# A decode-and-prompt hybrid layer: sample queries computed as rows, a third key place from the start, scores half a sample further ahead, gate sigmoids after the sample loop

## What is computed

```python
h = rms_norm(x, g_norm1) * (1.0 + sc1) + sh1
proj = h @ w_in        # q|k|v (8 heads x 64), glu_a|glu_b (512 each), gate_a|gate_c (1024 each)
q = rms_norm(q.reshape(B, S, 8, 64), g_q)      # k likewise with g_k
attn = moba_attention(q, k_all, v_all, pos0, alibi_slopes()) @ w_attn_proj   # top-3 past blocks of 256 keys, plus the own block
u = glu_a * sigmoid(glu_b)
cv = silu(layer_norm(depthwise_conv31(u))) @ w_conv_proj
mix = (sigmoid(gate_a) * attn + sigmoid(gate_c) * cv) @ w_out
x = x + gt1 * mix
# then: second norm, SwiGLU with 2816 hidden channels, gated residual
```

## Time and profile before

| | us |
|---|---|
| median of three runs | 590.48 (588.69 to 595.14) |
| time of the profiled execution | 588.94 |
| its span, first to last instruction | 587.2 |
| projections, from q's landing to the loop | 39 to 104 |
| loop over samples | 104 to 286 for b = 0 to 6, then sample 7 |
| PE busy | 528.6 (90%) |
| DVE busy | 394.7 (67%) |
| ACT busy | 291.6 (50%) |
| POOL busy | 169.7 (29%) |

### The profile page before, as it was taken

The page is one execution under the profiler, slowest core; times in us unless marked ns, Lnnn a source line. Parts: engine busy times, 40 slices in busy tenths (PEclk is TensorE's granted clock), DMA queues, the critical chain, the costliest instruction groups (busy, mean ns, idle before and its releaser), DMA issues.

```text
span 587.2 us, 10410 instructions
## 1 busy us (share of the span) xinstructions
PE 528.6 (90%) x4180; PEld 447.7 (76%) x4180; DVE 394.7 (67%) x602; ACT 291.6 (50%) x519; POOL 169.7 (29%) x232
## 2 busy tenths in 40 slices
PE   3869899888888989889888999899999999999997
PEld 3658778765474756657548888789999999999996
DVE  1652773889899999998766864567566656554441
ACT  3144444686777768664563532284344444434331
POOL 8325377386768668660100000000000000000000
PEclk9589899988979979897979999999999999999999
DMA  8999459599999999999586989947466445466501
GB/s 306 367 371 398 147 205 361 215 367 341 389 387 385 397 372 419 360 362 415 201 337 219 386 291 376 367 142 237 144 205 218 153 150 162 129 185 168 159 20 38
DMA packets 82128, 159.31 MB, mean 271 GB/s; under 512 B 2573, under 2 KB 61113, under 8 KB 76952
## 3 DMA queue, kind: packets, MB, share of 16 engines
q1 hardware_dynamic: 76256, 89.27, 45.5%
q0 software_dynamic: 5120, 67.71, 29.1%
q10 hardware_dynamic: 703, 1.67, 0.8%
HBM read 156.39 MB, written 2.72 MB: 271 GB/s over the span
## 4 chain that ended last, share of the span: by engine, by line
PE 62%; DVE 19%; DMA 5%; ACT 5%; issue 5%; POOL 2%; SPq 1%; ACTq 1%; DVEq 0%; POOLq 0%
PE acc L1580 12%; PE acc L1581 12%; PE acc L1582 12%; PE acc L1452 7%; DVE prod L1057 5%; DVE sall L1064 3%; DMA wring<-in_w_ffn_in 2%; PE acc L1465 2%; PE acc L1467 2%; PE acc L1466 2%; PE acc L1384 2%; DMA pr<-in_page_table 2%; DMA wring<-in_w_in 2%; PE chain L1604 1%; ACT L623 1%
## 5 line engine op out<-in xcount | busy, mean ns | idle before, releaser
L1129 DVE TENSOR_TENSOR wlo<-wring,whi 128x1024 fp32r<-128x1024 f32 (+2 forms) x84 | 92.0, 1097 | 72.1 <-ACT whi L623 71.3
L623 ACT ACTIVATE whi<-wring 128x1024 fp32r<-128x1024 f32 (+2 forms) x84 | 80.1, 958 | 83.1 <-PE acc L1582 77.2
L1580 PE MATMUL acc<-xlo,whi 128*128 128x264 f32 x384 | 110.2, 287 | 3.5 <-DVE wlo L1129 1.3
L1581 PE MATMUL acc<-xhi,wlo 128*128 128x264 f32 x384 | 108.8, 283 | 0.0
L1582 PE MATMUL acc<-xhi,whi 128*128 128x264 f32 x384 | 108.8, 283 | 0.0
L1452 PE MATMUL acc<-hT,wring 128*128 128x264 f32 x336 | 99.3, 447 | 2.7 <-DMA wring<-in_w_in 2.3
L578 POOL TENSOR_TENSOR cvT<-cvT,cprod 128x256 f32<-128x256 f32 x120 | 87.7, 731 | 45.4 <-ACT cprod L623 30.7
L1452 PEld LDWEIGHTS acc<-hT,wring 128*128 128x128 f32 x336 | 70.5, 220 | 21.2 <-issue 4.4
L1580 PEld LDWEIGHTS acc<-xlo,whi 128*128 128x128 f32 x384 | 72.3, 188 | 5.8 <-issue 3.1
L1064 DVE TENSOR_REDUCE sall<-prod 128x32 f32<-128x2048 f32 x32 | 73.0, 2280 | 0.4
L1581 PEld LDWEIGHTS acc<-xhi,wlo 128*128 128x128 f32 x384 | 72.4, 188 | 0.1
(11 more groups left out here) (316 smaller groups left out, 909.6 us busy)
## 6 DMA issues: line engine op xcount, KB each, us to landing
wring<-in_w_ffn_in SPq DMA_DIRECT2D x22, 1024.0 KB, 7.6
wring<-in_w_ada SPq DMA_DIRECT2D x20, 1024.0 KB, 14.5
wring<-in_w_in SPq DMA_DIRECT2D x12, 1024.0 KB, 9.0
wring<-in_w_ffn_out SPq DMA_DIRECT2D x16, 704.0 KB, 5.6
more<-in_w_out SPq DMA_DIRECT2D x4, 1024.0 KB, 13.7
more<-in_w_ada SPq DMA_DIRECT2D x4, 1024.0 KB, 12.4
wring<-in_w_in SPq DMA_DIRECT2D x6, 512.0 KB, 12.0
wring<-in_w_in SPq DMA_DIRECT2D x4, 768.0 KB, 13.6
```

The costliest lines, as they stand in the source:

```text
L623: return nc.scalar.activation(out, in_, f, **kw)
L1129: v.tensor_tensor(wlo[:, place, 0:n, :], w, whi[:, place, 0:n, :].bitcast(F32), ALU.subtract)\
L1580: mm(bank[:, 0:R], whi[:, place, k - k0, :], lo[:, k, :], start=k == 0, stop=False)
L1581: mm(bank[:, 0:R], wlo[:, place, k - k0, :], hi[:, k, :], start=False, stop=False)
```

## The change

It does six things.

1. The samples' query rows come from a product of their own, eight products with the eight input columns as the stationary side (128 x 8) and q's weights (128 x 512) as the moving side, into four groups of rows of `chain`; ACT copies them, one product with a selector `rowsel` adds the four groups into rows 0 to 7 and again into rows 32 to 39 of `psS`; ACT squares them, DVE sums by head and multiplies with the gain (`grow`), ACT takes the root, DVE scales (`qfull`), ACT and DVE split. `spread_query(0)` stands in the middle of q1, `spread_query(1)` after k0. The old way (`halves` product, transposes) is gone.
2. `PLACE` gives q, v to place 1 and k, glu to place 0; place 2 holds keys from the start. v now waits for q3's products, glu for k3's.
3. `gather_k(0)` is issued when q's weights have landed; the later ones each come earlier by position, one more ahead of the loop (chunks 0 to 5 instead of 0 to 4).
4. Six score steps (0,0) to (1,1) precede the loop, instead of four and a multiplication; in the loop a turn does steps 4b+6 to 4b+9. PE's block sums of turn b now also wait for `p_ready` of turn b-1.
5. `gate(n)` is a copy; four `open_gates` calls (four tiles each) apply the sigmoid in place after turn 7: one ahead of `values(7)`, one behind it, two at units 3 and 7. DVE waits for `gates_open` before a `cp` or `ap` bank.
6. `spread_norm` uses three banks and is placed after v2 (three) and after a0 (three).

```diff
-PLACE = dict(zip(SLOTS, [0, 1, 2, 0, 1, 2, 0, 1] + [n % 2 for n in range(B - 1)]))
-PLACE.update(conv=2, attn=1, mod4=0, mod5=0, out0=3, mod6=2, out1=4, mod7=0, mod8=2, mod9=0, mod10=3, mod11=4)
-PLACE.update({name: (1, 2, 0)[n % 3] for n, name in enumerate(x for x in SLOTS if x[0] == "f")})
+PLACE = dict(zip(SLOTS, [0, 1, 2, 0, 1, 0, 1, 0] + [(n + 1) % 2 for n in range(B - 1)]))
+PLACE.update(conv=2, attn=0, mod4=1, mod5=1, out0=3, mod6=2, out1=4, mod7=1, mod8=2, mod9=1, mod10=3, mod11=4)
+PLACE.update({name: (0, 2, 1)[n % 3] for n, name in enumerate(x for x in SLOTS if x[0] == "f")})
...
@@ POOL @@
+            pool.wait_ge(w_full[PLACE["q"]], 32 * LOADS["q"])
+            gather_k(0)
+            pool.wait_ge(qpart_ready, 1)
             for name in ON_POOL:
                 rest(name)
-                if name == "q1":
-                    gather_k(0)
-                if name == "k0":
+                if name == "q3":
                     gather_k(1)
+                if name == "k2":
+                    pool.wait_ge(ada_used, 3)
+                    gather_k(2)
                 if name == "v0":
-                    pool.wait_ge(acc_full, NUMBER[LAST_FILL["k"]] + 1)
-                    gather_k(2)
+                    gather_k(3)
+                if name == "v1":
+                    gather_v(0, 0)
                 if name == "v2":
-                    gather_k(3)
-                if name == "v3":
-                    gather_v(0, 0)
-                if name == "b1":
                     gather_k(4)
+                if name == "a0":
+                    gather_k(5)
...
-                gather_k(CH * b + 5)
+                gather_k(CH * b + 6)
                 add_taps(b, 2)
-                gather_k(CH * b + 6)
+                gather_k(CH * b + 7)
@@ ACT @@
+            input_high(0)
+            input_high(1)
+            act.wait_ge(qpart_ready, 1)
+            func(pvm[:, :], chain[:, :], ACT.Copy).then_inc(qpart_copied, 1)
+            for t in range(2, 5):
+                input_high(t)
+            act.wait_ge(qrow_ready, 1)
+            func(qsq, psS[both, :], ACT.Square).then_inc(qsq_ready, 1)
+            for t in range(5, KD):
+                input_high(t)
+            act.wait_ge(qss_ready, 1)
+            func(qroot, qss, ACT.Sqrt, scale=1.0 / DH, bias=eps[both, :]).then_inc(qroot_ready, 1)
             high("q2")
+            act.wait_ge(qfull_ready, 1)
+            func(qsplit[both, :], qfull, ACT.Copy).then_inc(qs_ready, 1)
...
-                freed(func(gates[:, n, :], bank[:, 0:R], ACT.Sigmoid), f"g{n}")
+                freed(func(gates[:, n, :], bank[:, 0:R], ACT.Copy), f"g{n}")
+
+            def open_gates(first):
+                for n in range(first, first + 4):
+                    wait_freed(act, f"g{n}")
+                func(gates[:, first:first + 4, :], gates[:, first:first + 4, :], ACT.Sigmoid).then_inc(gates_open, 1)
...
+            open_gates(8)
             values(B - 1)
+            open_gates(12)
...
+                if n_unit in (3, 7):
+                    open_gates(n_unit - 3)
@@ DVE @@
+            dve.wait_ge(qsq_ready, 1)
+            v.tensor_reduce(qss, qsq.rearrange(by_head, d=DH), AX.X, ALU.add).then_inc(qss_ready, 1)
+            at_gain = mark(v.tensor_tensor(qgain.rearrange(by_head, d=DH), psS[both, :].rearrange(by_head, d=DH),
+                                           grow.unsqueeze(1).to_broadcast([32 + B, H, DH]), ALU.mult))
+            input_low(3)
+            dve.wait_ge(qroot_ready, 1)
+            at_root = mark(v.reciprocal(qroot, qroot))
+            v.tensor_tensor(qfull.rearrange(by_head, d=DH), qgain.rearrange(by_head, d=DH),
+                            qroot.unsqueeze(2).to_broadcast([32 + B, H, DH]), ALU.mult).then_inc(qfull_ready, 1)
...
-            score(0, 0)
-            score(0, 1)
-            score(0, 2)
+            for half in range(STEPS):
+                score(0, half)
+            score(1, 0)
             dve.wait_ge(head_root, 1)
             v.reciprocal(headsums, headsums).then_inc(head_inv, 1)
-            score(0, 3)
-            for n in range(4):
-                head_norm(n)
-            dve.wait_ge(norm_read, 4)
-            v.memset(chain[:, :], 0.0).then_inc(chain_zero, 1)
-            multiply(1, 0)
-            for n in range(4, 6):
+            score(1, 1)
+            for n in range(6):
                 head_norm(n)
...
+                def multiply_next(slot):
+                    to, half = divmod(STEPS * b + 6 + slot, STEPS)
+                    if to < B:
+                        multiply(to, half)
...
-                if b >= 1:
-                    multiply_next(0)
+                multiply_next(0)
@@ PE @@
-            tile("q0", w, 0, hT)
-            split("q1")
+            pe.wait_ge(gs1_ready, 2)
+            for k in range(KD):
+                rows = slice(32 * (k % 4), 32 * (k % 4) + B)
+                ins = mm(chain[rows, :], hT[:, k, S:R], w[:, k, :], start=k < 4, stop=k >= 4)
+            ins.then_inc(qpart_ready, 1)
+            tile("q0", w, 0, hT, k1=2)
+            pe.wait_ge(qpart_copied, 1)
+            mm(psS[both, :], rowsel, pvm[:, :], start=True, stop=True).then_inc(qrow_ready, 1)
+            tile("q0", w, 0, hT, k0=2)
+            split("q1", k1=4)
+            pe.wait_ge(qs_ready, 1)
+            pe.wait_ge(qlo_ready, 1)
+            spread_query(0)
+            split("q1", k0=4)
...
-            spread_query(0)
-            split("k1", k0=3)
+            split("k0")
+            spread_query(1)
             head_sums(2)
+            split("k1")
...
                 pe.wait_ge(scored, STEPS * (b + 1))
+                if b >= 1:
+                    pe.wait_ge(p_ready, b)
```

More of the change, by code:

```diff
@@ L250, in program @@
         headsums = oT[0:2 * H, 0, :]
-        samples = pg[:, :, :].rearrange("p g h -> p (g h)")
-        qsn, qsq, qroot = (samples[:, 32 * e:32 * e + 32].rearrange("p (t b) -> p t b", t=4) for e in range(3))
-        wsel = samples[:, 96:96 + 30]
+        rowsel = pg[:, :, :].rearrange("p g h -> p (g h)")[:, 0:32 + B]
+        wsel = pg[:, :, :].rearrange("p g h -> p (g h)")[:, 96:96 + 30]
+        both = slice(0, 32 + B)
+        grow = s1[both, :, :].rearrange("p g h -> p (g h)")[:, 0:DH]
+        qss, qroot = (s1[both, :, :].rearrange("p g h -> p (g h)")[:, DH + 8 * e:DH + 8 * e + 8] for e in range(2))
+        qsq = cvT[both, :, :].rearrange("p t r -> p (t r)")[:, 0:A]
+        qgain, qfull = (oT[both, 2 * e:2 * e + 2, :].rearrange("p t r -> p (t r)")[:, 0:A] for e in range(2))
         rowsq, rowfac = tiny[:, 0:3], tiny[:, 4:7]
@@ L274, in program @@
         spread_factor = small[:, 0:R]
-        normbank = [psS, psT, chain, small, psS, psT]
+        normbank = [psS, psT, small]
         sums_, gate_, mask_, turned_ = small[:, 0:QU], small[0:H, 8:8 + NB], small[:, 0:P], small[0:H, P:2 * P]
@@ L543, in _ @@
                                      channel_multiplier=1))
+            step(g.memset(rowsel, 0.0))
+            step(g.tensor_copy(rowsel[:, 0:H], headof[:, :]))
+            step(g.tensor_copy(rowsel[:, 32:32 + H], headof[:, :]))
             step(g.memset(wsel, 0.0))
@@ L687, in _, with input_high @@
             high("q1")
-            for t in range(KD):
+            def input_high(t):
                 act.wait_ge(h_ready, min(t + 1, H_BY_DVE))
@@ L701, in _ @@
             high("k1")
+            square("q", 2)
             raw("q", 3)
[L703 to L709 removed]
             square("q", 3)
+            high("k2")
             raw("k", 0)
[L712 to L717 removed]
             square("k", 0)
@@ L1545, in _ @@
             head_sums(7)
-            spread_query(1)
             split("v1")
             split("v2")
-            split("v3", k1=4)
-            for n in range(4):
+            for n in range(3):
                 spread_norm(n)
-            split("v3", k0=4)
-            for n in range(4, 6):
+            split("v3")
+            split("a0")
+            for n in range(3, 6):
                 spread_norm(n)
-            split("a0")
             split("b0")
```

86 lines of the change are left out of this document (37 added, 49 removed).

## The result

| | before | after |
|---|---|---|
| median (10 runs each, same chip) | 592.22 us (588.69 to 596.34) | 598.43 us (594.38 to 604.07) |
| profiled execution, its span, its clock | 588.94, 587.2, 0.945 | 601.15, 599.4, 0.934 |
| start of the loop, DVE's copy to `gsT` of sample 0 | 104.30 | 119.78 |
| turns 0 to 6 together | 182.0 | 177.9 |
| from sample 7's `gsT` to the end of the span | 300.9 | 301.7 |

The change makes the kernel slower: ratio 1.0116, 95% interval 1.0083 to 1.0148. (Ratios are of undisturbed runs, so they differ a little from the quotients of the medians.) The forecast was 584.1 with a range to 591.5. The two profiled executions stand 12.2 us apart, more than the medians (6.2), and the table divides that: 15.5 lost ahead of the loop, 4.1 won in it, 0.8 lost behind it.

What follows compares the result with a forecast made beforehand. It took PE to bound the projections, DVE the loop and PE turn 6; -1.6 - 2.6 - 0.9 + 0.3 = -4.8 on 588.94 gave 584.1 us. Its own range was 580.1 to 587.3, the 8-in-10 range 577.5 to 591.5.

Steps and rivals of the forecast that it cites:

- part 1: Projections, from q's weights landing at 38.98: end 1.6 us earlier; bounds a loss of 0.3, a gain of 3.5.
- Rival C: Ahead of the loop: two weight places are too few, v lands late and PE waits; 589.9 to 591.8 us; chance 0.13.
- Part 2: Loop, turns 0 to 5: DVE's waits for ACT in turns 1 and 3 shrink, 2.6 us gained; bounds 1.3 and 4.7.
- Part 3: Turn 6: DVE loses two steps, but only PE's own waits fall, 0.9 us gained; bounds 0.5 and 4.4.
- rival A: PE keeps full clock in turn 6 and sigmoid waits of turns 2 and 4 partly go; 579.6 us; chance 0.22.
- Part 4: After the loop: the first `open_gates`, ahead of `values(7)`, costs 0.3 us; bounds 0 and 1.4.
- Rival B: Loop: the DMA engines hold it, so its 2.6 us of gain are lost; 586.7 us; chance 0.13.

Runs made afterwards that it cites:

- e1: Changed kernel with four gathers kept until glu's weights have landed; 591.37 us, ratio 0.9994 to the kernel before.
- e7: Changed kernel with the first gather of values behind a0's remainder and key chunk 5 behind b0's; 589.0 us (one run).
- e9: Changed kernel, two weight places kept, with e7's order of gathers and POOL's remainder of q3 held until DVE's of q2; 587.76 us, ratio 0.9932.
- e11: Repeat of e6: changed kernel with three weight places, POOL's remainder of q3 held until DVE's of q2; 585.33 us, ratio 0.9908.
- e5: Kernel before plus gate sigmoids behind the loop and scores half a sample ahead, chunk 5 gathered behind the first taps; 590.16 us, ratio 1.0006.
- e2: Changed kernel with the old three weight places, gathers moved to suit, head norms' reciprocal ahead of `score(1, 0)`; 586.59 us, ratio 0.9948.
- e4: Changed kernel with glu read as one block of 512 columns, so it computes with wrong columns; 595.63 us (one run).
- e6: As e2, with POOL's remainder of q3 held until DVE's remainder of q2 is done; 583.84 us, ratio 0.9884 to the kernel before.
- e10: e6 without the scores half a sample ahead, so scores as before the change; 586.02 us, ratio 0.9923 to the kernel before.

## Why the prediction was wrong

**The step that failed** is the sentence "glu's, at 73, is wanted after 85. Hidden" in part 1. The load was issued at 78.5 and wanted at 91, and it took 24.2 us: a stall of 11.8 on ACT, 8.7 on PE, and half clock behind it. e1 and e7 show that the gathers beside it are the cause, and the packets show how. The prediction had named the rule of the page "DMA: Bandwidth & Descriptors" of the Trainium skill, Queues, rings and completion order, that engines take turns packet by packet, and then read it as half rate, and only for v's load beside one gather. Turns are by packet: 366 to 380 in after, 398 to 432 with wider reads. With 15 KB against 1 KB, half the packets are a fifteenth of the bytes. The landings of before didn't show that, as none of those loads ran beside three gathers; the 17.3 us elsewhere, of a load in the loop, were the warning. The rule held in these traces; what was missing beside it were the two packet sizes, which the trace of the kernel before could have given.

**Rival C** had the right resource and the wrong victim: it priced v's landing and took 11.5 us as the time from which it decides. v came through in after, in 7.5 us; glu, with three gathers instead of one beside it, did not. v's turn came in e9, with 13.5 us to land and 1.5 of wait, near the 2.0 that rival C's threshold gives.

**Part 1, projections, -1.6.** The new product took 3.60 (3.6 taken), the selector's product 1.06 (0.9), `spread_query(0)` came at 51.05 where 50.0 was forecast and PE had started 0.76 later. The order and its prices were right, as e11 shows: k2 at 66.68 against 66.7, from a first product 0.5 later. (But 1.7 us of the gain against before are the clock, as said above: without the fall behind the old wait the old way, in e5, was as fast to k2.) Missing was DVE's subtraction of q2, 3.40 instead of 1.2, beside POOL's: 1.91 of wait, and with the slower clock behind it 3.5 us in after. e1, e2, e4 and e7 had the same wait without the slower clock, so 1.9 is its own price. Before the change DVE's started at 45.46, half a microsecond ahead of POOL's; now it stands behind the query chain, at 51.63, just behind the start of POOL's for q3. The prediction gave this subtraction no term of its own and never asked what POOL ran at its new place. One of its bounds is also added up wrongly: 1.6 + 0.8 + 1.8 is 4.2 and not 3.5. Nothing in the result hangs on that.

**Part 2, turns 0 to 5, -2.6.** Measured -2.9 in after and -3.8 with the gates alone. Turns 1 and 3 gave 1.2 and 0.8 in after, less than the 1.73 and 0.86 of the forecast. Turn 2 gave 1.1 that was not forecast, its waits of 0.70 and 0.42 shrinking to one of 0.19, and turn 0 gave 0.5; turns 4 and 5 became longer by 0.4 and 0.2. The sum fits better than its terms, and that is in part luck.

**Part 3, turn 6, -0.9.** Measured -1.2, at a granted clock of 0.86 against 0.87 in before. In e5, e6 and e11 turn 6 was 3.6 us shorter than in before, at 1.00, and in e4, which has after's program but for glu's read, 2.9 shorter, at 0.93. So rival A's mechanism exists, and what turn 6 takes goes with its clock, which nothing here forecasts. PE did hold the turn, and DVE waited 9.8 us in four places.

**Part 4, after the loop, +0.3.** Measured +0.8, within its bounds.

**Rival B** fell: no wait of DVE in the loop of after was for keys. The full DMA engines did not hold the gathers up there, they held up the loads that share the engines with them. (In e5, where chunk 5 was issued late, DVE did wait 2.97.)

So the parts in and behind the loop came to -3.3 against the forecast's -3.2, and the error lies wholly ahead of the loop: +15.5 in the profile against -1.6. By the table above some 10.7 of the 17.1 us between them are glu's load, 1.9 the subtraction of q2, 0.8 a later first product, and most of the rest the clock.

## What to carry to other kernels

Whether a transfer is hidden depends on what shares the DMA engines with it. Take every queue that is active from its issue to its landing, give each the same number of packets, and only then turn packets into bytes: here the queue with small packets got a fifteenth of the bytes. When work is moved in time on one engine, look at what the other engines now run beside it, not only at who waits for it. A freed resource (here a third place for keys) is paid for by what had it before: here glu's load was issued at 54.02 for a use at 88, and after the change at 78.51 for one at 91.

## What the runs showed of the hardware

- Weight loads in packets of 1 KB beside gathers in packets of 15 KB on average moved 0.39 MB in 14 us (28 GB/s), alone 0.3 to 0.35 MB a us (0.61 in 2 us in e7, 0.69 from 80 to 82 in after). Packets of 2 KB got 0.88 MB in 16 us (e4). A gather's first packets came 4.5 us behind its issue in after, glu's own 1 us behind; the difference is the head start that a load has.
- A subtraction of two SBUF tiles on DVE and one on POOL did not overlap: the one that started second took 3.40 instead of 1.22 us (DVE, in after) and 2.97 instead of 2.4 (POOL, before).
- PE's granted clock in after was 1.00 from 60 to 93 us, 0.50 from 93.5 to 96.6 while PE worked without a wait, 1.00 again, and 0.50 from 100 to 111, from within the wait of 8.73 on. e1, e7 and e9, too, fell to 0.50 for some 3 us from 91 on with PE at work; their last waits before that were of 0.9 us, at 84 to 85. Behind the wait of 1.91 it was 0.50 from 56 to 59 in after and stayed at 1.00 in e1, e2, e4 and e7. e6 had 1.00 from 36 to 105.
- Executions of one kernel differ by 10 us and more, mostly with the clock: e6 gave 577.6 at 0.961 and 589.1 at 0.942. But e10 gave 583.9 at 0.950 and 595.2 at 0.957, so the mean clock is not all of it. A single profile can't rank these kernels.
